# Gates and branches of a hybrid decoder block formed feature-major, with ScalarE adding the gate's bias

## The reference

```
h = rms_norm(x, norm_pre_w);  proj = h @ w_in           # 1024 x (8 * 1024 + 16 + 2 * 1024)
qkv_a, z_a, beta_a, dec_a, qkv_b, z_b, gate_logits = split(proj)
ya = rms_norm(gated_delta_rule(silu(conv(qkv_a)), ...)) * silu(z_a)     # 8 heads of 128
yb = moba_attention(qkv_b) * silu(z_b)                                  # 8 heads of 128
gates = sigmoid(gate_logits + b_gate)                   # 256 x 2 x 1024
merged = gates[:, 0] * (ya @ w_branch[0]) + gates[:, 1] * (yb @ w_branch[1])
out = x + rms_norm(merged @ w_out, norm_post_w)
```

## Time and profile before

| | |
|---|---|
| median of three runs | 357.48 us |
| profiled execution | 357.55 us |
| its span, first to last instruction | 355.8 us |
| PE busy | 347.6 us (98% of the span) |
| DVE busy | 270.0 us (76%) |
| ACT busy | 218.8 us (62%) |
| POOL busy | 58.7 us (16%) |

### The profile page before, as it was taken

How to read it: one execution, slowest core, us unless ns; L and a number is a source line. 1 busy time by engine, 2 the same in 40 slices (tenths; PEclk the granted TensorE clock), 3 DMA queues, 4 the chain that set the end, 5 groups by cost and what they waited for, 6 DMA issues and landing times.

```text
span 355.8 us, 6674 instructions
## 1 busy us (share of the span) xinstructions
PE 347.6 (98%) x2387; PEld 318.4 (89%) x2387; DVE 270.0 (76%) x551; ACT 218.8 (62%) x483; POOL 58.7 (16%) x114
## 2 busy tenths in 40 slices
PE   7999999999999999999999999999999999999993
PEld 5889998888899999999999999999998888888882
DVE  3869897599997868978788797878977656566744
ACT  5877894542457667686867766777676544425421
POOL 1534436500050000301103020030301101000011
PEclk9999999999999999999999999999999999999999
DMA  8667948793698485446745565465534735766423
GB/s 264 178 193 194 334 158 270 198 329 119 167 257 228 121 214 141 121 122 164 188 120 128 145 178 147 120 164 145 165 121 138 247 118 172 254 226 236 124 113 118
DMA packets 76206, 63.48 MB, mean 178 GB/s; under 512 B 4724, under 2 KB 62478, under 8 KB 76174
## 3 DMA queue, kind: packets, MB, share of 16 engines
q1 hardware_dynamic: 73838, 59.37, 57.3%
q0 software_dynamic: 1152, 3.30, 3.1%
q10 hardware_dynamic: 1184, 0.39, 0.5%
HBM read 61.46 MB, written 1.59 MB: 177 GB/s over the span
## 4 chain that ended last, share of the span: by engine, by line
PE 84%; DVE 8%; DMA 3%; issue 2%; ACT 1%; POOL 0%; DVEq 0%; SPq 0%; ACTq 0%; POOLq 0%
PE banks L1395 40%; PE banks L1450 15%; PE banks L1657 6%; PE banks L1413 6%; DVE w_lo L919 3%; DVE sub L1061 2%; DMA xin<-in_x_dram 1%; DMA raw<-in_w_in_dram 1%; DMA sub<-m_blocks 1%; PE banks L1545 1%; PE banks L1523 1%; PE banks L1562 1%; PE banks L1551 1%; PE banks L1380 1%; DVE sub L1063 1%
## 5 line engine op out<-in xcount | busy, mean ns | idle before, releaser
L919 DVE TENSOR_TENSOR w_lo<-raw,w_hi 128x1024 fp32r<-128x1024 f32 x102 | 123.8, 1220 | 42.3 <-ACT w_hi L670 41.6
L670 ACT CAST w_hi<-raw 128x1024 fp32r<-128x1024 f32 x103 | 107.2, 1047 | 30.0 <-PE banks L1450 12.3
L1395 PE MATMUL banks<-h_hi,w_hi 128*128 128x256 f32 x440 | 64.0, 288 | 0.2 <-DVE acc L989 0.2
L1395 PE MATMUL banks<-h_lo,w_hi 128*128 128x256 f32 x440 | 59.4, 277 | 0.0
L1395 PE MATMUL banks<-h_hi,w_lo 128*128 128x256 f32 x440 | 59.3, 277 | 0.0
L1395 PEld LDWEIGHTS banks<-h_hi,w_hi 128*128 128x128 f32 x440 | 55.2, 189 | 0.7 <-DVE acc L989 0.3
L1395 PEld LDWEIGHTS banks<-h_hi,w_lo 128*128 128x128 f32 x440 | 54.2, 188 | 0.0
L1395 PEld LDWEIGHTS banks<-h_lo,w_hi 128*128 128x128 f32 x440 | 54.2, 188 | 0.0
L989 DVE SCALAR_TENSOR_TENSOR acc<-banks,vec,acc 128x255 f32<-128x255 f32 (+2 forms) x72 | 34.5, 480 | 3.7 <-ACT acc L790 1.5
L616 POOL TENSOR_TENSOR so<-so,rnq 128x2 f32<-128x2 f32 x8 | 2.0, 251 | 162.8 <-ACT junk L857 162.8
L790 ACT ACTIVATE acc<-banks,vec 128x256 f32<-128x256 f32 x16 | 7.6, 473 | 17.4 <-PE banks L1395 17.4
(11 more groups left out here) (258 smaller groups left out, 607.6 us busy)
## 6 DMA issues: line engine op xcount, KB each, us to landing
raw<-in_w_in_dram SPq DMA_DIRECT2D x80, 512.0 KB, 4.9
raw<-in_w_branch_dram SPq DMA_DIRECT2D x16, 512.0 KB, 4.7
raw<-in_w_out_dram SPq DMA_DIRECT2D x8, 512.0 KB, 4.2
xin<-in_x_dram SPq DMA_DIRECT2D x2, 512.0 KB, 3.8
th_E<-g_rows POOLq DMA_DIRECT2D x2, 512.0 KB, 7.2
bias<-bias_rows POOLq DMA_DIRECT2D x1, 1024.0 KB, 7.5
raw<-in_x_dram SPq DMA_DIRECT2D x2, 512.0 KB, 3.7
out_dram<-xin SPq DMA_DIRECT2D x4, 256.0 KB, 2.0
```

Of the source, the lines that this page charges most:

```text
L670: nc.scalar.copy(w_hi[:, t % SLOTS, :], raw[:, t % SLOTS, :]).then_inc(s_hi, 1)
L919: v.tensor_tensor(w_lo[:, t % SLOTS, cols], raw[:, t % SLOTS, cols], w_hi[:, t % SLOTS, cols].bitcast(F32), ALU.subtract).then_inc(s_lo, 1)
L1395: last = mm(ps, w, r, start=part == 0 and k == 0, stop=part == 2 and k == KT - 1)
```

## The change

Gates and branches take the feature-major form of the heads' tiles: `third` in place of `group_third`, banks 0 and 1 in turn, one tile for 128 features. The gate's bias is then a value per partition: it comes in with the other small vectors at the start (one more small DMA, turned by the same transpose of PE) and ACT adds it in the tanh itself, from PSUM (`gate_tanh`, 16 times 256 wide). The bias rows, their four DMAs and DVE's additions go. DVE's product with the gate, the sum, and both parts of m are now done per tile of 128 features; the sum has its features on the partitions as it stands, so `turn_m` goes. `bd_lo` moves behind the larger buffers, whose addresses stay. The loads of gates and branches become 1024 rows of 128 columns.

```diff
@@ scalar
+            def gate_tanh(g):
+                n = GATES_A + g if g < EARLY else GATES_B + g - EARLY
+                sa.wait_ge(s_tile, n + 1)
+                if g == 0:
+                    sa.wait_ge(s_vec, 3)
+                ac(gate(g), bank[n % 2][:, 0:SEQ], ACT.Tanh, bias=bgate[:, g:g + 1], scale=0.5).then_inc(s_gate_th, 1)
+            def m_part(k):
+                sa.wait_ge(s_m_sum, k + 1)
+                nc.scalar.copy(m_hi[:, k:k + 1, :], one(gate(KT + k))).then_inc(s_m_hi, 1)
...
+                for g in range(2 * KT):
+                    if S == 3 * (GATES_A + g if g < EARLY else GATES_B + g - EARLY) + 3:
+                        gate_tanh(g)
+                for k in range(KT - 1):
+                    if S == 3 * (BRANCH0 + KT + k) + 4:
+                        m_part(k)
                 if part == 1:
                     split_hi(n + LEAD, n + LEAD, (n + LEAD) // SLOTS + 1)
+            m_part(KT - 1)
             for k in range(KT - LEAD):
                 split_hi(OUT0 + k + LEAD, k + LEAD, (OUT0 + k + LEAD) // SLOTS + 1)
-                if k == 2:
-                    for b in range(2):
-                        m_parts(1, b)
@@ vector
+            def second_branch(k):
+                n = BRANCH0 + k
+                ve.wait_ge(s_gate_th, KT + k + 1)
+                ve.wait_ge(s_tile, n + 1)
+                v.scalar_tensor_tensor(out=gate(KT + k), in0=gate(KT + k), scalar=1.0, in1=bank[n % 2][:, 0:SEQ],
+                                       op0=ALU.add, op1=ALU.mult).then_inc(s_m_b, 1)
+            def first_branch(k):
+                n = BRANCH0 + KT + k
+                ve.wait_ge(s_tile, n + 1)
+                v.scalar_tensor_tensor(out=gate(k), in0=gate(k), scalar=1.0, in1=bank[n % 2][:, 0:SEQ],
+                                       op0=ALU.add, op1=ALU.mult).then_inc(s_m_a, 1)
+                ve.wait_ge(s_m_b, k + 1)
+                ve.wait_ge(s_m_a, k + 1)
+                v.tensor_tensor(gate(KT + k), gate(KT + k), gate(k), ALU.add).then_inc(s_m_sum, 1)
+            def m_rest(k):
+                ve.wait_ge(s_m_hi, k + 1)
+                v.tensor_tensor(m_lo[:, k:k + 1, :], one(gate(KT + k)), m_hi[:, k:k + 1, :].bitcast(F32),
+                                ALU.subtract).then_inc(s_m_lo, 1)
...
+                for k in range(KT):
+                    if S == 3 * (BRANCH0 + k) + 3:
+                        second_branch(k)
+                    if S == 3 * (BRANCH0 + KT + k) + 3:
+                        first_branch(k)
+                    if S == 3 * (BRANCH0 + KT + k) + 5:
+                        m_rest(k)
                 if part == 2:
                     split_lo(n + LEAD, n + LEAD)
-            first_branch(1)
+            first_branch(KT - 1)
             for k in range(KT - LEAD):
                 split_lo(OUT0 + k + LEAD, k + LEAD)
-                if k == 2:
-                    m_rest(1)
+                if k == 0:
+                    m_rest(KT - 1)
@@ tensor
+                elif n < GATES_B + 2:
+                    pe.wait_ge(s_gz, 2 * HEADS - 1 + n - GATES_B)
+                elif n < BRANCH0 + 2:
+                    pe.wait_ge(s_gate_th, EARLY + n - GATES_B - 1)
+                elif n < BRANCH0 + KT + 2:
+                    pe.wait_ge(s_m_b, n - BRANCH0 - 1)
+                else:
+                    pe.wait_ge(s_m_a, n - BRANCH0 - KT - 1)
...
             for k in range(KT - SLOTS):
                 pe.wait_ge(s_hi, OUT0 + k + 1)
                 pe.wait_ge(s_lo, lo_done(OUT0 + k))
-                if k == 0:
-                    pe.wait_ge(s_m_lo, 2)
+                pe.wait_ge(s_m_lo, k + 1)
                 for c in range(NC):
                     for e in range(2):
                         last = out_products(k, c, e)
                 last.then_inc(s_tile, 1)
-                if k == 1:
-                    turn_m(1)
```

More of the change, by code:

```diff
@@ L441, in _ @@
                 first_load(n)
[L442 to L446, removed]
             for g in range(EARLY):
-                gate_load(GATES_A + g, g // 4, g % 4)
+                load(GATES_A + g, GATES_A + g, w_tile(COL_GATE + P * g))
             for h in range(HEADS):
@@ L634, in _ @@
             for g in range(HEADS):
[L635 to L638, removed]
                 o_norm(g)
@@ L1207, in branch_done @@
-            def branch_done(group, c):
-                if c == 0:
-                    ve.wait_ge(s_branch_p, group + 1)
-                else:
-                    ve.wait_ge(s_tile, BRANCH0 + 4 * group + 4)
-            def second_branch(half):
-                ve.wait_ge(s_gate_th, (3, 4)[half])
-                for c in range(NC):
-                    branch_done(half, c)
-                    part = th[2 + half][:, c, :]
-                    v.scalar_tensor_tensor(out=part, in0=part, scalar=1.0, in1=branch_banks[half][c], op0=ALU.add,
-                                           op1=ALU.mult).then_inc(s_m_b, 1)
@@ L1224, in first_branch @@
-            def first_branch(half):
-                if half:
-                    ve.wait_ge(s_m_turned, 1)
-                for c in range(NC):
-                    branch_done(2 + half, c)
-                    part = th[half][:, c, :]
-                    v.scalar_tensor_tensor(out=part, in0=part, scalar=1.0, in1=branch_banks[2 + half][c], op0=ALU.add,
-                                           op1=ALU.mult).then_inc(s_m_a, 1)
-                    ve.wait_ge(s_m_a, 2 * half + c + 1)
-                    ve.wait_ge(s_m_b, 2 * half + c + 1)
-                    v.tensor_tensor(m_tok[c], th[2 + half][:, c, :], part, ALU.add).then_inc(s_m_sum, 1)
@@ L1436, in bank_free @@
                         pe.wait_ge(s_bT, 2 * h + t - 3)
-            def group_third(n, part, left_hi, left_lo, banks, done):
-                q, slot = n % 4, n % SLOTS
-                if part == 0:
-                    pe.wait_ge(s_hi, n + 1)
-                elif part == 2:
-                    pe.wait_ge(s_lo, lo_done(n))
-                for kk in range(2):
-                    for c in range(NC):
-                        left = (left_lo if part == 1 else left_hi)[:, 2 * q + kk, P * c:P * c + P]
-                        right = (w_lo if part == 2 else w_hi)[:, slot, 512 * kk:512 * kk + 512]
-                        last = mm(banks[c], left, right, start=q == 0 and kk == 0 and part == 0,
-                                  stop=q == 3 and kk == 1 and part == 2)
-                        if q == 3 and kk == 1 and part == 2 and c == 0:
-                            last.then_inc(done, 1)
-                if part == 2:
-                    last.then_inc(s_tile, 1)
@@ L1493, in turn_m @@
-            def turn_m(half):
-                pe.wait_ge(s_m_sum, 2 * half + 2)
-                if half == 0:
-                    pe.wait_ge(s_gate_b, 8)
-                for k in range(4):
-                    for c in range(NC):
-                        last = tp(m_banks[half][k // 2][:, SEQ * (k % 2) + P * c:SEQ * (k % 2) + P * c + P],
-                                  m_tok[c][:, P * k:P * k + P], ident)
-                last.then_inc(s_m_turned, 1)
+                elif n < GATES_B + 2:
[4 more added lines that the diff above has]
+                    pe.wait_ge(s_m_b, n - BRANCH0 - 1)
+                else:
+                    pe.wait_ge(s_m_a, n - BRANCH0 - KT - 1)
@@ L1644, in _ @@
                     value_third(n, part)
-                elif GATES_A <= n < HEAD0 or GATES_B <= n < BRANCH0:
-                    gate_third(n, part)
                 elif n >= BRANCH0:
-                    branch_third(n, part)
+                    branch = 1 - (n - BRANCH0) // KT
+                    if part == 0:
+                        bank_free(n)
+                        if n == BRANCH0:
+                            pe.wait_ge(s_ylo_b, HEADS)
+                        elif n == BRANCH0 + KT:
+                            pe.wait_ge(s_ylo_a, HEADS)
+                    third(n, n, part, y_hi[:, branch], y_lo[:, branch])
                 else:
```

136 lines of the change are left out of this document (22 added, 114 removed).

## The result

The changed kernel took 359.96 us (median of 6 runs, 358.88 to 361.44), the kernel before 357.57 (357.46 to 357.59) beside it: ratio 1.0069, 95% interval 1.0048 to 1.0090. Timed again, beside the kernel before, it took 359.62 against 357.69, ratio 1.0057 (1.0036 to 1.0078). The forecast was 357.7 with a range to 359.1: the time lies outside the range, and a clear loss had been given a chance of 0.31.

The account below looks back on a forecast made before the run. PE's own stream was taken to set the end. Tiles -0.5, entry -0.65 and loop +1.37 (transposes' removal included) gave +0.2 us on 357.55; with the median 0.07 lower, 357.7 us, range 356.0 to 359.1.

Parts of the forecast that it names:

- Narrower tiles: Gate and branch tiles as 24 matmuls of 256 columns: 0.02 us less per tile, -0.5 us over 25 tiles.
- rival 4: Gate and branch tiles: the narrow form is slower by losing an overlapped 0.17 us per third, +16 us, 374 us; chance 0.02.
- The turning: Branch products: two sets of 8 transposes leave PE's stream, worth 1.6 us, 1.8 with slower first matmuls behind them.
- The loop: Tiles 88 to 98: DVE and ACT steps in series make PE wait 3.2 us; +1.37 us against before.
- Rival 1: Tiles 88 to 95: the loop over DVE and ACT does not bind, 354.3 us; chance 0.15.
- Rival 2: Output projection: the late loop delays the loads of tiles 102 and 103, PE waits, 358.6 us; chance 0.13.
- Rival 3: Gate stage: PE waits for ACT's tanh of two tiles before, 0.1 us in 16 tiles, 359.3 us; chance 0.06.
- Entry of the head stage: Tiles 28 to 31: PE's wait for DVE's late convolution goes with the bias-row additions, -0.65 us, bounds 0 and -0.7.
- The turn of the loop: Tiles 88 to 95: six links over DVE and ACT sum to 3.425 us per tile, bounds 3.35 and 3.55.
- The start: Kernel start: one more small DMA delays the first weight tile, covered by DVE's 0.76 us idle; at worst +0.3 us.

Follow-up runs that it names:

- e7: e2 with both sets of eight transposes put back into PE's stream, their result unused: 357.97 us, ratio 1.0009 to the kernel before.
- e2: Changed kernel with ACT's high part of m put behind the rounding of the weights of tile n+3: 356.13 us, ratio 0.9952 to the kernel before.
- e6: Changed kernel with ACT forming each high part of m twice, in series: 363.51 us, ratio 1.0163 to the kernel before.
- e10: Changed kernel with DVE's rest of m put behind the low part of the weights of tile n+3: 362.26 us, ratio 1.0136 to the kernel before.
- e5: Changed kernel with the edits of e2 and e3 together: 354.63 us, ratio 0.9920 to the kernel before.
- e3: Changed kernel with ACT's tanh of gate tiles put behind the rounding of tile n+3: 358.64 us, ratio 1.0028 to the kernel before.
- e8: Changed kernel with the 1 MB bias table's load held until DVE's low part of tile 23 is done: 358.75 us, ratio 1.0032 to the kernel before.
- e9: e5 with the bias table's load issued late as in e8: 354.73 us, ratio 0.9925 to the kernel before.

## Why the prediction was wrong

What bounds the kernel was read rightly: PE's stream, and whatever makes PE wait. So were these:

- **Narrower tiles.** 12 gate tiles gained 0.31 us in all eleven profiles, 0.026 each for 0.02 said. The 13 of tiles 76 to 88 gained less, some 0.08 together (the shift of tile 89 against tile 76), so the term of -0.5 was -0.4. 24 matmuls of 256 columns in 2.722 us are 113 ns each. The sustained spacing in the Trainium skill ("TensorE: Matmul & The Clock Gate", Back-to-back issue gap) would, by the prediction's estimate, have made the 32 tiles some 12 us slower; this trace does not agree with it, and rival 4 is out.
- **The turning**, priced at 1.8 and measured at 2.06 in the profiles of e7 and e2.
- **The loop**: its place, its links, who waits and where. By the distances of its tile starts over 2.72 us, PE lost 0.3 before tile 93, 0.8 before each of 94 and 95, 0.5 before 96 and 0.8 before each of 97 and 98, 4.0 us for 3.2 said. e2, e6 and e10 show that it sets the end. Rival 1 is out, by 3.5 us; its 354.3 us is what the kernel reaches once the loop and the entry are cured (354.6 in e5). Rival 2 is out here, with no wait behind tile 98, and shows in e10, where the loop turns 0.34 us slower. Rival 3 is out as it stood: PE never waited for the tanh itself.

Two terms fell short, and each by something that can be named; a third held:

- **The step "Entry of the head stage", -0.65.** This is the step that failed. It was +0.03 in the profile near the median and +0.79 in the other, and +0.09 in the middle of seven profiles. I had seen that the rounding queues behind a tanh that waits for its tile, and had settled it with "it keeps about 0.5 us of reserve at tile 31". That counted only the rounding's own lateness. It left out that the low part behind it is also what releases a pair of loads (the same link that I followed in rival 2, at the other end of the kernel), and that a load issued later meets another transfer. A wait of 0.95 us on ACT became some 1.3 us on the issue in both profiles, once PE's own lateness is taken off, and 1.4 to 2.0 us on DVE. e3 gives it back in one way, e8 in another, and e9 shows that they are one. Also the tanh takes 0.48 us and not the 0.38 of its like in the earlier trace rows; here it carries a bias per partition, the nearest row did not. Size of the miss: 0.7 to 0.8 us at the median.
- **The turn of the loop, 3.425, was 3.51.** The links again, from DVE's and ACT's rows above: product to sum 0.51, sum to high part 0.46, high part to rounding 0.31, rounding to low part 1.09, low part to product 1.14. All but the first are within 0.02 of what I took. I had 0.03 for the gap between product and dependent sum, from a pair of 512 columns; behind one of 256 it is 0.10. Over seven turns and the last way through to tile 98 the turn's 0.09 makes 8 x 0.09 = 0.7: tiles 89 to 98 took 28.47 us for 27.75 said, +2.09 instead of +1.37. The bound of 3.55 had held it.
- **The start, 0 with an upper bound of +0.3, held.** At tile 9 the eleven profiles lie between -0.10 and +0.27, +0.05 in the mean. The +0.27 is the second profile's, which has this wait of PE:

```profile
PE banks L1242 <- DMA y<-in_dn_onorm_w_dram: 0.8, 1, 0.8
```

Together: 357.7 + 0.7 (entry) + 0.7 (loop) + 0.1 (tiles) = 359.2. The second profile (359.63) has 0.3 more, from its own first 16 tiles. Either of the two misses alone, 358.4, would have stayed within the range; both together left it. My range took in each bound by itself but not their sum: entry at 0, loop at 3.55 and start at 0.3 give 359.6 as well. What I had no term for is the late decay table, +1.4 in three of eleven profiles, which is in the longest run (361.44). The second profile lost 2.1 us against before without it, so it does not decide the sign, and its cause stays open, as said.

## What to carry to other kernels

Before moving a step ahead of another on an in-order engine, write down the loop that it closes: each instruction that waits for another engine, what stands behind it in program order, and whether that in turn releases the first. The turn of such a loop is a sum of latencies, to be held against the bounding engine's time per tile; here 3.51 against 2.72 us, with DVE 66% and ACT 34% busy in that stretch, and one exchange of two instructions made the 0.6% loss a gain. And where a step that might be late also releases a load, follow the load: its reserve is not that of the engine.

## What the runs showed that I had not expected

- A 256-wide instruction of DVE whose successor reads its result cost 0.51 us start to start for 0.41 of length; the 512-wide pair before the change cost 0.72 for 0.69. Halving the width cut the work by 40% and not the gap.
- Of two 512 KB transfers on POOL's queue (the decay table) the page gives a landing of 8.0 us in one execution of a kernel and 7.2 in another, and PE waits 5 us behind it. The page's row on DMA issues (count, KB each, median us from issue to landing), first profile:

```profile
th_E<-g_rows POOLq DMA_DIRECT2D x2, 512.0 KB, 8.0
```

- A wait of PE costs 0.25 to 0.3 us more than the idle time that the profile names. Tile 94 starts 3.52 us after tile 93 for 2.72: 0.50 is named, 0.17 is the recorded tail of the matmuls ahead of the wait, over which the next one would have started, and 0.12 is the first group of eight behind it, which takes 1.19 us for 1.07 (the first 512-wide matmul 0.47 for 0.39). This is why the six waits of PE before tiles 93 to 98 add up to 2.4 us where the tile starts show 4.0.
